# First layer of a fused network kernel: queries and keys of latent attention as high and low parts, two score banks per step in differential attention, output weights split later, front in another order

## The reference, cut to what matters

```python
def diff_attend(q, k, v, lam, lam_init, out_g):
    s = jnp.einsum('bhiqd,bhikd->bhiqk', q, k) * (DA_DK ** -0.5)
    p = softmax_f32(s)
    a = p[:, :, 0] - lam * p[:, :, 1]
    o = jnp.einsum('bhqk,bhkd->bhqd', a.astype(v.dtype), v)
    return rms_norm(o, out_g) * (1.0 - lam_init)

def mla_attend(qn, qr, kn, kr, v):
    s = (jnp.einsum('bhqd,bhkd->bhqk', qn, kn) + jnp.einsum('bhqd,bkd->bhqk', qr, kr)) * ((MLA_NOPE + MLA_ROPE) ** -0.5)
    p = softmax_f32(s)
    return jnp.einsum('bhqk,bhkd->bhqd', p.astype(v.dtype), v)

hx = modulate(rms_norm(x, norm_mix_g[l]), sh_a, sc_a)
y_x, y_c = even_mixer(hx, hc, need_ctx, ...)
x = x + g_a * (y_x @ w_out[l])
```

## Time and profile before

| | |
|---|---|
| median of 3 runs | 2473.31 us (2471.73 to 2475.14) |
| the profiled execution: its time | 2472.95 us |
| its span in the trace | 2471.2 us |
| TensorE matmuls (PE) | 2316.3 us busy, 94% |
| VectorE (DVE) | 1514.4 us, 61% |
| ScalarE (ACT) | 1019.5 us, 41% |
| first 300 us of the span | the first layer up to its output projection |

### The profile page before, as it was taken

The page is one execution under the profiler, slowest core; times in us unless marked ns, Lnnn a source line. Parts: engine busy times, 40 slices in busy tenths (PEclk is TensorE's granted clock), DMA queues, the critical chain, the costliest instruction groups (busy, mean ns, idle before and its releaser), DMA issues.

```text
span 2471.2 us, 33032 instructions
## 1 busy us (share of the span) xinstructions
PE 2316.3 (94%) x14198; PEld 1993.9 (81%) x14198; DVE 1514.4 (61%) x1866; ACT 1019.5 (41%) x1223; POOL 0.2 (0%) x4
## 2 busy tenths in 40 slices
PE   6978989999998978999999998999999999899997
PEld 3755667777777757999898876899989987689997
DVE  3877453333356586554777766665678766757475
ACT  4246442121224155433564434444455534444343
POOL 0000000000000000000000000000000000000000
PEclk9999999999998999999999999999999999999999
DMA  7440134444332141555554553445445545444542
GB/s 316 171 170 1 52 143 164 187 154 188 118 119 101 70 103 69 188 178 197 192 196 175 183 181 116 170 180 188 180 179 200 180 170 191 141 154 171 184 177 101
DMA packets 61113, 389.19 MB, mean 157 GB/s; under 512 B 6568, under 2 KB 11048, under 8 KB 15784
## 3 DMA queue, kind: packets, MB, share of 16 engines
q1 hardware_dynamic: 60968, 387.08, 43.2%
HBM read 386.01 MB, written 1.05 MB: 157 GB/s over the span
## 4 chain that ended last, share of the span: by engine, by line
PE 83%; DVE 9%; ACT 3%; issue 3%; DMA 2%; SPq 0%; DVEq 0%; ACTq 0%
PE PS L479 25%; PE PS L480 25%; PE PS L481 25%; DMA raw<-chunks_in 1%; PE PS L929 1%; ACT w_hi L1131 1%; PE PS L783 1%; DVE w_lo L1559 1%; PE PS L626 1%; PE PS L665 1%; DVE stat L1754 1%; PE PS L911 1%; PE PS L690 1%; ACT xn L1209 1%; DVE BIG L1763 1%
## 5 line engine op out<-in xcount | busy, mean ns | idle before, releaser
L1559 DVE TENSOR_TENSOR w_lo<-raw,w_hi 128x2048 fp32r<-128x2048 f32 x300 | 684.3, 2290 | 537.3 <-ACT w_hi L1131 535.4
L1131 ACT ACTIVATE w_hi<-raw 128x2048 fp32r<-128x2048 f32 x300 | 572.0, 1912 | 766.3 <-PE PS L481 456.4
L479 PE MATMUL PS<-x_hi,w_hi 128*128 128x256 f32 (+1 forms) x2048 | 631.9, 309 | 22.7 <-DVE x_lo L1643 9.7
L480 PE MATMUL PS<-x_lo,w_hi 128*128 128x256 f32 (+1 forms) x2048 | 628.9, 307 | 0.0
L481 PE MATMUL PS<-x_hi,w_lo 128*128 128x256 f32 (+1 forms) x2048 | 628.3, 307 | 0.0
L479 PEld LDWEIGHTS PS<-x_hi,w_hi 128*128 128x128 f32 x2048 | 396.2, 193 | 49.3 <-issue 22.1
L480 PEld LDWEIGHTS PS<-x_lo,w_hi 128*128 128x128 f32 x2048 | 396.0, 193 | 16.7
L481 PEld LDWEIGHTS PS<-x_hi,w_lo 128*128 128x128 f32 x2048 | 395.9, 193 | 16.7
L479 PE MATMUL PS<-w_hi,x_hi 128*128 128x512 f32 (+1 forms) x800 | 317.3, 397 | 22.6 <-DVE w_lo L1559 10.6
L480 PE MATMUL PS<-w_lo,x_hi 128*128 128x512 f32 (+1 forms) x800 | 313.4, 392 | 0.0
L481 PE MATMUL PS<-w_hi,x_lo 128*128 128x512 f32 (+1 forms) x800 | 313.1, 391 | 0.0
(11 more groups left out here) (284 smaller groups left out, 2267.7 us busy)
## 6 DMA issues: line engine op xcount, KB each, us to landing
raw<-chunks_in SPq DMA_DIRECT2D x348, 1024.0 KB, 4.8
bias_ring<-brows_in SPq DMA_DIRECT2D x32, 256.0 KB, 5.0
G<-nrows_in SPq DMA_DIRECT2D x2, 1536.0 KB, 6.6
free_b<-rel_in SPq DMA_DIRECT2D x4, 512.0 KB, 7.7
BIG<-rel_in SPq DMA_DIRECT2D x4, 512.0 KB, 8.6
tabt<-tabs_in SPq DMA_DIRECT2D x1, 1536.0 KB, 12.3
X<-x_in SPq DMA_DIRECT2D x1, 1024.0 KB, 8.5
X<-ctx_in SPq DMA_DIRECT2D x1, 1024.0 KB, 10.5
```

The source lines that it names most:

```text
L479: pe.matmul(o, lhs[0], rhs[0], start=start, stop=False, **more)
L480: pe.matmul(o, lhs[0], rhs[1], start=False, stop=False, **more)
L1131: act.activation(w_hi[:, i % HI_RING, :], ring[:, n % RING, :], ACT.Copy).then_inc(*hi_ready.now(n))
L1559: dve.tensor_tensor(w_lo[:, c % RING, :], ring[:, c % RING, :], w_hi[:, i % HI_RING, :].bitcast(F32), ALU.subtract).then_inc(*lo_ready.now(c))
```

## The change

- Latent attention: the turned queries and keys (`qnT`, `qrT`, `knT`, `krT`) are stored as high and low parts. ScalarE copies each turned block as the high part, VectorE subtracts for the low part, for all ten blocks and the rope key. A unit's scores are now six single-pass matmuls.
- Differential attention: score banks rotate by two units, banks of turned probabilities and of values by two (0 and 6, 1 and 7). TensorE's order is turn(u), scores(u+2), values(u-1). VectorE takes both reciprocals in one instruction in `norms`, and none in `outs`.
- The splits of the first two chunks of `w_out` move from the place ahead of differential attention into latent attention, behind units 3 and 6 on ScalarE, and 4 and 7 on VectorE.
- The split of the `ukv` chunk moves ahead of the evictions of `uq` on ScalarE.
- Front: the fifth adaLN chunk runs between the sums and the broadcast of the first norm; VectorE makes the low part of the first projection chunk ahead of the first low part of x.

```diff
-    return (2 + 2 * (u % 3), 0, 1, u % 3) if ph == "da" else (4 + u % 4, u % 2, 2 + u % 2, u % 4)
+    return (2 + 2 * (u % 2), 6 * (u % 2), 1 + 6 * (u % 2), u % 3) if ph == "da" else (4 + u % 4, u % 2, 2 + u % 2, u % 4)
...
-            mla.append(dict(scores=[[(v["qnT"][:, h, q], v["knT"][:, h, k0:k0 + nk]),
-                                     (v["qrT"][part, h // 2, q], v["krT"][part, k0:k0 + nk])]],
+            pairs = [([a[:, h, q] for a in v["qnT"]], [a[:, h, k0:k0 + nk] for a in v["knT"]]),
+                     ([a[part, h // 2, q] for a in v["qrT"]], [a[part, k0:k0 + nk] for a in v["krT"]])]
+            mla.append(dict(scores=[[(a[x], b[y]) for a, b in pairs for x, y in ((0, 0), (0, 1), (1, 0))]],
...
-            add("mlakr", 1, 4, lambda b: v["krT"])
-            add("qn", 4, 4, lambda b: v["qnT"][:, b, :])
+            add("mlakr", 1, 4, lambda b: v["krT"], kind="parts")
+            add("qn", 4, 4, parts(v["qnT"]), kind="parts")
...
                 mm.then_inc(*sums_bc.now(key))
+                if meanwhile:
+                    meanwhile()
                 pe.wait_ge(*rstd_diag.after(key))
...
                 for u in range(len(us)):
+                    if ph == "da":
+                        turn_probs(u)
                     if u + 2 < len(us):
                         scores(u + 2)
                     if u >= 1:
                         values(u - 1)
-                    turn_probs(u)
+                    if ph == "mla":
+                        turn_probs(u)
...
-            root_of_squares(("mix", 0), 4, 0)
-            for _ in range(4):
+            root_of_squares(("mix", 0), 4, 0, mod_chunk)
+            for _ in range(3):
                 mod_chunk()
...
             root(("dak", 0), 16, 64)
+            split_to(first_ev + 7)
             for t in range(4):
-                if t == 2:
-                    split_to(first_ev + 7)
-                    root(("dak", 1), 16, 64)
...
             modulation(2)
-            split_to(first_ev + 11)
+            split_to(first_ev + 9)
...
             def dao_root(u):
                 if u in range(2, 14, 3):
                     root(("dao", u // 3), 4, 128)
+                if u in (3, 6):
+                    split_to(first_ev + 9 + u // 3)
...
-                    link(dve.reciprocal(r, stat[:, o + 1:o + 2]))
+                    link(dve.reciprocal(stat[:, o + 8:o + 10], stat[:, o:o + 2]))
...
                 maxes(0)
                 maxes(1)
+                norms(0)
                 for u in range(len(us)):
-                    norms(u)
                     if u + 2 < len(us):
                         maxes(u + 2)
+                    if u + 1 < len(us):
+                        norms(u + 1)
...
-            norm_mod(("mix", 0), 4, KD, (0, 0), lambda k: lo_to(ev) if k == 0 else None)
+            norm_mod(("mix", 0), 4, KD, (0, 0), None, lambda: lo_to(ev))
...
-            lo_to(ev + 11)
             modulation(0, 1)
...
             def dao(u):
                 h = u // 3
+                if u in (4, 7):
+                    lo_to(ev + 9 + u // 3)
```

More of the change, by code:

```diff
@@ L584, in sum_of_squares, with root_of_squares @@
                 reader[b] = std_ready.after(key)
-            def root_of_squares(key, tiles, bank=7):
+            def root_of_squares(key, tiles, bank=7, meanwhile=None):
                 acc, n = sums[tiles][0], tiles * P
@@ L642, in turn_halves @@
                     mm.then_inc(*turned.now(key, b))
-                    reader[bank] = (copied_s if b % 2 else copied_v).after(key, b)
+                    reader[bank] = copied_v.after(key, b)
             def await_copies(key, nb):
@@ L850, in even_mixer @@
                 turn("kn", 4, 4, lambda b, t: k_l0[:, t, b, :])
-                await_copies("mlakr", 1)
-                for k in ("qn", "qr", "kn"):
-                    await_copies(k, copies[k][0])
+                for k in ("mlakr", "qn", "qr", "kn"):
+                    pe.wait_ge(*copied_v.after(k, copies[k][0] - 1))
                 attend("mla")
@@ L1333, in _ @@
             copy_turned("mlac")
+            copy_turned("mlakr")
             root(("daq", 0), 16, 64)
@@ L1345, in _ @@
                                ACT.Copy).then_inc(*stored_s.now("uq", 0, t, 0))
+            root(("dak", 1), 16, 64)
             split_to(first_ev + 8)
@@ L1602, in inverse_root, with norm_mod @@
                 link(dve.reciprocal(r, r))
-            def norm_mod(key, tiles, lead=2, mod=None, at_tile=None):
+            def norm_mod(key, tiles, lead=2, mod=None, at_tile=None, ahead=None):
                 whos, n = tiles // 2, tiles * P
@@ L1629, in norm_mod @@
                     modulation(*mod)
+                if ahead:
+                    ahead()
                 for k in range(KD):
@@ L1723, in outs @@
                     d, b = us[u], attention_banks(ph, u)[2]
-                    o, r = 200 + 2 * (u % 4), stat[:, 212 + u % 4:213 + u % 4]
-                    dve.wait_ge(*exp_ready.after(ph, u))
-                    link(dve.reciprocal(r, stat[:, o:o + 1]))
+                    o = 200 + 2 * (u % 4)
+                    r = stat[:, o + 8:o + 9]
+                    if ph == "mla":
+                        dve.wait_ge(*exp_ready.after(ph, u))
+                        link(dve.reciprocal(r, stat[:, o:o + 1]))
                     dve.wait_ge(*attended.after(ph, u))
```

15 lines of the change are left out of this document (8 added, 7 removed).

## The result

| | before | after |
|---|---|---|
| median | 2473.31 us | 2495.06 us (2494.14 to 2500.11, 5 runs) |
| span of the profiled execution | 2471.2 us | 2493.3 us |
| TensorE matmuls busy | 2316.3 us | 2327.6 us |
| mean granted clock of TensorE | 0.976 | 0.968 |

The changed kernel is slower: the ratio is 1.0091, 95% interval 1.0077 to 1.0106. The prediction was 2474.0 with a range of 2464 to 2481, and gave "slower" 0.17.

A forecast was written before the change was run, and what follows sets the result against it. The prediction took TensorE, 94% busy, as the bound, so gains had to come where it waits or works too long. Terms -4.4 - 1.1 - 9.1 + 14.0 + 0.7 + 1.0 = +1.1 on 2472.95 gave 2474.0 us, range 2464 to 2481.

The forecast's parts named there:

- signs of being wrong: Differential attention under 50 us, latent attention under 42, or the clock row dropping between 170 and 225 us.
- signs of being right: First projection near 36.3 us, queries turned 12 to 13 us earlier, differential attention 54 to 56 us, latent attention about 46.
- Front, -4.4: Before the first projection: TensorE starts it at about 36.3 us instead of 40.8, carried on; 4.4 us won, bounds 2.3 and 6.5.
- Split of the second latent chunk: Ahead of four evictions on ScalarE: VectorE no longer waits for the split; 1.1 us won, bounds 0 and 2.
- Output weights later, -9.1: Ahead of differential attention: queries turned at 168.1 us and faster transposes; 9.1 us won, bounds 7.1 and 9.6.
- Differential attention, +14: Differential attention: turn, scores, maximum and mixing become one serial loop of 55.2 us; 14 us more, bounds 11 and 17.
- rival 3: Differential attention: the clock falls to 1.2 GHz for half of 47 us, +11, kernel 2485 us; chance 0.12.
- Turns, +0.7: Turns ahead of latent attention: ten blocks need a copy and then a subtraction, 7.4 us against 6.75; 0.7 more.
- Latent attention, +1: Latent attention: 9.6 us of saved products outweighed by ScalarE's string, splits and copies; about +1, bounds -9.6 and +4.
- Rival 1: Latent attention stays bound by TensorE, so the 9.6 us are won; kernel 2464 us, chance 0.15.
- Rival 2: Differential attention: the loop doesn't close because score matmuls overlap the mixing; kernel 2460 us, chance 0.04.
- rival 4: Front: the load is held by the queue ahead, winning 1 us instead of 4.4; kernel 2477.4 us, chance 0.05.

The follow-up runs named there:

- sixth kernel: The kernel before with the re-ordered front alone; 2473.66 us, ratio 0.9995.
- fourth kernel: The changed kernel with the split of the second latent chunk, and the root behind it, back between the second and third eviction of the queries on ScalarE; 2489.94 us.
- fifth kernel: The kernel before with only the two output-weight splits and low parts moved into latent attention, products still 4-byte; 2474.59 us, ratio 1.0002.
- seventh: The kernel before with only the high and low parts of queries and keys for latent attention; 2475.07 us, ratio 1.0001.
- eleventh kernel: The kernel before with only the high and low parts for latent attention, TensorE waiting for the turned keys head by head; 2472.07 us, ratio 0.9994.
- second: The changed kernel with TensorE's old order in differential attention (scores, values, then turn) on the new banks; 2477.13 us, ratio to before 1.0015.
- third: The changed kernel with the old three pairs of score banks, one turn and one value bank, and TensorE's new order; 2496.56 us.
- first kernel: The kernel before with the new differential attention alone (banks, TensorE's order, doubled reciprocal); 2492.36 us, ratio 1.0081.

## Why the prediction was wrong

The profiled execution came out 21.0 us above the sum of the terms. By stage, 5.5 are missing up to the last adaLN chunks, 0.5 in the output weights, 4.1 in differential attention, 1.3 in the turns, 6.7 in latent attention, and 2.9 behind the layer. Of the prediction's own signs of being wrong, one came: the clock row drops between 170 and 225 us. Of its signs of being right, one failed clearly: the queries are turned 6.6 us earlier (168.67 for 175.22), not 12 to 13.

1. *Front, -4.4.* Right as far as 112 us: 36.87 us for a forecast of 36.3, and 4.0 us ahead. That it would be carried to the end was assumed. Part of the 4.0 is the late trace of the kernel before. The first product of the latent keys starts at 128.4 to 130.1 us in the five kernels with the old front (130.1 is the kernel before), and at 126.0 to 126.8 in the six with the new front and the old place of the split: nearer 3 than 4. In the changed kernel the next step took it, and alone it brought nothing that the medians show (sixth kernel).
2. *Split of the second latent chunk, -1.1, bounds 0 and 2.* This step failed. It asked who waits for the split, and not what is queued behind it, and took for granted that its chunk had landed when ScalarE came to it. The landing was at 116.8 us, the evictions stood behind it, and the 4.0 us of the front were lost, 0.7 in longer idles and 3.3 in products at the lower clock behind them. The prediction had the evictions free because the third tile "stood idle there anyway". It did not: before, TensorE has no idle from the first product of the latent queries at 116.9 us to the adaLN chunk at 125.4, and its idle of 3.60 us stands behind that, ahead of the keys. The idle of the third tile, 2.29 us, came with the change. The fourth kernel got 3.6 us back. A bound of "nothing" on the side of a loss had no row behind it.
3. *Output weights later, -9.1.* Right in size: 8.6 us at the first scores, 9.2 alone (7 to 8 beside the kernels that are not late there). What the step left out, the price at the new place, was in the step on latent attention, and too small there.
4. *Differential attention, +14.* The mechanism of the loop was right in every part. A head takes 13.7 us at full clock, from 199.15 to 212.88 us, as worked out; VectorE's maximum waits in every unit; with TensorE's old order the loop is gone, and with three pairs of banks it stays. The size came out at 18.1, because rival 3 happened beside it.
5. *Rival 3, the clock, chance 0.12.* Partly right: the clock was at 0.50 to 0.66 in about 15 of the 59 us and cost about 4 (58.8 measured against the 55.2 worked out for full clock; the five steps from 178.52 to 199.15 us take 20.6 us, where the sum for full clock has 16.9); 11 were priced. The evidence against it, a full clock at 2.84 busy us of 5, was too thin. In the window ahead of the fall TensorE was busy for 1.81 us of 5, and stood idle for 3.19 us at one place; an idle of 1.91 follows. The prediction had the start-up of 5.2 us in its own sum and did not ask what the clock does in it. (Before, an idle of 2.75 us at the same place had left the clock up. That was luck of the trace: the fifth, sixth and seventh kernels, with the same instructions in this stage, show a mean clock of 0.96 in it and the kernel before 1.00.) The Trainium skill, "TensorE: Matmul & The Clock Gate", section "A second HAM failure mode: psum-queue depth-cycling", has the clock swing between its levels where TensorE idles briefly between groups. Here it did in the first 26 us of the stage, with one window at 1.00 between them; from 199 us on, with the same pattern of idles, it stayed at 1.00. So the trace agrees with the rule for one part of the stage only.
6. *Turns, +0.7.* 2.0. One of the two is the wait at the end, 1.94 us for VectorE's low parts where 0.88 had been for a copy; most of the other is two waits for a subtraction before a bank is free, 0.55 and 0.22 us.
7. *Latent attention, +1, bounds -9.6 and +4.* This step failed most. Turns and stage together cost 9.7 us more, and the experiments divide them: parts, arranged so that TensorE doesn't wait, -3.1 (50.2 us in the eleventh kernel against 53.3 of the kernel before); the idle ahead of the first scores and the clock after it, +8.1 (58.3 in the seventh against 50.2); the splits, +4.7 (fifth kernel). The sum is 9.7. That it fits so well is partly luck: the second, third and fourth kernels have the same instructions in this stage as the changed one, and took 55.8, 55.9 and 57.3 us for its 54.2. Three sizes were off:
   - The 9.6 us of saved products were never there. It compared 2.08, the duration of a group to its last modelled end, with 6 x 0.23, an interval between starts. By one view, the chain, the scores of 512 keys take 1.91 us as 4-byte products and 1.59 as six single passes, those of 256 keys 1.06 and 0.90. That is 0.96 us per head and 3.8 in all. Chain of waits of the kernel before:

```profile
238.30 1.91 PE PS L665 x4
...
244.29 1.06 PE PS L665 x4
```

   The Trainium skill, "FP8 and Floating Point Precision", section "TensorE Precision Notes", gives four passes for a true FP32 product. Two products are then eight passes, and the trace agrees with 1.91 us, 8 x 0.24. The prediction quoted this rule and went by its own 4.5; the runs side with the rule. The saving that it worked out by the rule, 5.6 us, was still too large, because the six single passes take 1.59 us and not 6 x 0.23.
   - The clock. The prediction watched for it in differential attention alone. Here an idle of 1.9 us was followed by a fall in five traces of five.
   - The splits, priced as ScalarE's lump alone; VectorE's low part and sums are in the same string.
8. *The rest.* Rival 1 priced a saving that did not exist: even with nothing in TensorE's way the stage took 43.4 us, 3 under before. Rival 2 is ruled out by the 15 waits, rival 4 by the 4.0 us at 112 us. The chance of "slower" rested on the sum of many terms with ends that were too near. Three terms failed, all to the side of a loss: the latent chunk, the clock in differential attention, and latent attention. The latent chunk and the two splits within latent attention failed for one reason: work that is moved has a price where it arrives.

## What to carry to other kernels

- On an engine that runs in order, ask of a moved instruction first what stands behind it and whether its own input will be there; a split that starts earlier, waits for a load and holds evictions back is worse here than a later one (4 us at the adaLN turn). Put such work where the engine has nothing ready: here two splits of 1.9 us with their low parts cost 5 us between table loads, and nothing at the two ends of the same stage.
- Where engine A turns, scores and hands over, and engine B takes maxima and mixes, let A issue the next scores ahead of the turn that waits for B. Three calls in another order were 18 us.
- A wait for a whole set of copies, of which the first is enough to begin with, costs its idle and then the slow clock behind it. Waiting by head was worth 8 us between two traces, and 3.0 between the medians.

## What the runs showed of the hardware

- An idle of TensorE of about 2 us, after a stretch of short transposes, was followed by 13 us at 1.2 GHz (0.50 in two whole windows of 5 us); the same products without the idle ran at 2.4 GHz. That held in five traces with the idle and three without it. What an idle does is not settled by its length alone: 2.75 us left the clock at 1.00 in the kernel before, and 3.19 us at the same place were followed by 0.50 in the changed one. Nor is it settled by the instructions: an idle of 3.57 to 3.60 us ahead of the latent keys' first product stands in eleven kernels, with the same products of TensorE around it. In the kernel before, the clock stayed at 1.00 up to 140 us; in the other ten a window of 5 us in that stretch has 0.50 to 0.79. A single trace can't tell whether such an idle costs a fall.
- With the serial loop the stage took 57.6, 58.8 and 62.6 us in three kernels with the same instructions in it (first kernel, changed kernel, fourth), with a mean granted clock of 0.91, 0.88 and 0.78; with the old bank numbers it took 63.7 us at 0.79 (third). One profiled execution gives the size of such a stage to a few microseconds only.
- Six single-pass products of 512 columns take 1.59 us in a row of the chain, 0.265 each, where long runs of them take 0.23: small groups pay for their first product (0.32 us to the second, in the group at 277.65 us of after).
